# A decoder trunk on one core: the Strassen-like blocks of the down projection asked for earlier, spaced five groups apart, with VectorE's work cut smaller and the sums of h on GpSimd

## The reference

```python
g = x @ w_gate;  u = x @ w_up                    # 2048 -> 5632
gc = conv_b + sum(conv_w[j] * gp[:, j:j + S])    # three causal taps
y = (silu(gc) * u) @ w_down                      # h (256 x 5632) times w_down, 5632 -> 2048
x = layer_norm(ALPHA * x + y, ln2_g, ln2_b)
```

## Time and profile before

| | us |
|---|---|
| median of 3 runs | 2232.48 (2232.12 to 2232.66) |
| the profiled execution, its own time | 2233.07 |
| span of the profiled execution | 2231.0 |
| TensorE busy | 2204.4 |
| VectorE busy | 1531.2 |
| ScalarE busy | 1073.2 |
| GpSimd busy | 242.6 |

### The profile page before, as it was taken

How to read it: one execution, slowest core, us unless ns; L and a number is a source line. 1 busy time by engine, 2 the same in 40 slices (tenths; PEclk the granted TensorE clock), 3 DMA queues, 4 the chain that set the end, 5 groups by cost and what they waited for, 6 DMA issues and landing times.

```text
span 2231.0 us, 28589 instructions
## 1 busy us (share of the span) xinstructions
PE 2204.4 (99%) x11370; PEld 1882.7 (84%) x11370; DVE 1531.2 (69%) x2034; ACT 1073.2 (48%) x1405; POOL 242.6 (11%) x250
## 2 busy tenths in 40 slices
PE   9999999999999999999999999999999999999998
PEld 7888888888888888778888888888888888887787
DVE  6655676786667666787685566767866666677876
ACT  5444555444444445444354445554444444455443
POOL 1751000220000000000008410002200000000000
PEclk9999999999999999999999999999999999999999
DMA  8655565666666666656665554755666666666565
GB/s 276 194 169 161 152 217 176 184 190 191 189 191 190 191 189 210 195 170 198 209 193 169 162 165 146 226 177 182 189 189 189 190 190 190 191 216 194 162 199 186
DMA packets 210213, 420.94 MB, mean 189 GB/s; under 512 B 13056, under 2 KB 15136, under 8 KB 209056
## 3 DMA queue, kind: packets, MB, share of 16 engines
q1 hardware_dynamic: 207216, 406.37, 58.8%
q0 software_dynamic: 2432, 12.22, 1.6%
q10 hardware_dynamic: 432, 0.52, 0.1%
HBM read 416.97 MB, written 2.10 MB: 188 GB/s over the span
## 4 chain that ended last, share of the span: by engine, by line
PE 92%; DVE 5%; DMA 2%; issue 0%; SPq 0%; ACT 0%; POOLq 0%; POOL 0%; DVEq 0%
PE ps L1489 29%; PE ps L1493 15%; PE ps L1375 13%; PE ps L1377 13%; PE ps L1376 13%; DMA sraw<-in_w_down_dram 2%; DVE slo L1054 1%; DVE wlo L914 1%; PE ps L1539 1%; PE ps L1541 1%; PE ps L1540 1%; PE ps L1420 1%; PE ps L1638 1%; PE ps L1612 1%; DVE xres L1000 1%; PE ps L1589 1%
## 5 line engine op out<-in xcount | busy, mean ns | idle before, releaser
L914 DVE TENSOR_TENSOR wlo<-raw,whi 128x1024 fp32r<-128x1024 f32 x731 | 927.0, 1276 | 521.7 <-ACT whi L647 516.0
L647 ACT ACTIVATE whi<-raw 128x1024 fp32r<-128x1024 f32 x731 | 769.4, 1059 | 738.8 <-DMA raw<-in_w_up_dram 216.9
L1489 PE MATMUL ps<-xT,whi 128*128 128x512 f32 x2816 | 657.3, 390 | 0.0
L1489 PEld LDWEIGHTS ps<-xT,whi 128*128 128x128 f32 x2816 | 522.4, 188 | 104.5 <-ACT qkT L668 0.4
L1375 PE MATMUL ps<-whi,xT 128*128 128x512 f32 x920 | 369.0, 401 | 0.0
L1377 PE MATMUL ps<-whi,xT 128*128 128x512 f32 x920 | 359.1, 390 | 0.0
L1376 PE MATMUL ps<-wlo,xT 128*128 128x512 f32 x920 | 358.2, 389 | 0.0
L1493 PEld LDWEIGHTS ps<-xT,wlo 128*128 128x128 f32 x2816 | 350.5, 192 | 7.5
L1493 PE MATMUL ps<-xT,wlo 128*128 128x256 f32 x2816 | 352.8, 283 | 0.0
L1375 PE MATMUL ps<-whi,hT 128*128 128x512 f32 x552 | 216.3, 392 | 4.7 <-DVE wlo L914 4.7
L1376 PE MATMUL ps<-wlo,hT 128*128 128x512 f32 x552 | 216.1, 391 | 0.0
(11 more groups left out here) (237 smaller groups left out, 1587.3 us busy)
## 6 DMA issues: line engine op xcount, KB each, us to landing
raw<-in_w_gate_dram SPq DMA_DIRECT2D x176, 512.0 KB, 4.0
raw<-in_w_up_dram SPq DMA_DIRECT2D x176, 512.0 KB, 4.0
raw<-in_w_in_dram SPq DMA_DIRECT2D x175, 512.0 KB, 3.7
raw<-in_w_down_dram SPq DMA_DIRECT2D x140, 512.0 KB, 4.2
raw<-in_w_out_dram SPq DMA_DIRECT2D x64, 512.0 KB, 4.2
sraw<-in_w_down_dram SPq DMA_DIRECT2D x36, 512.0 KB, 4.8
xres<-in_x_dram POOLq DMA_DIRECT2D x4, 512.0 KB, 5.9
lnb<-in_ln_g_dram POOLq DMA_DIRECT2D x2, 1024.0 KB, 8.1
```

The costliest lines, as they stand in the source:

```text
L647: act.activation(whi[:, s, :, :], raw[:, s, :, :], ACT.Copy).then_inc(hi_done, 1)
L914: dve.tensor_tensor(wlo[:, s, :, :], raw[:, s, :, :], whi[:, s, :, :].bitcast(F32), ALU.subtract)\
L1489: return pe.matmul(ps[:, bank, :], whi[:, s, kk, m * P:(m + 1) * P], xT[:, kt, :, :].rearrange("p a s -> p (a s)"), start=kt == 0, stop=kt ...
```

## The change

- `SETS_AT`: blocks 0 to 4 behind groups 9, 14, 19, 24, 29; blocks 5 to 8 behind 38, 43, 48, 53.
- The two loads of `sraw` for a block no longer wait for all seven products of the block in front: kk=1 waits for two of them, kk=0 for four. For this `set_used` counts products, S3 comes before S1, and each load has a semaphore.
- VectorE: `set_sum` is two parts, at `at+1` and `at+2`; `set_low` is two parts, of 2 at `at+2` and of 5 at `at+3`. ScalarE: `form_high` and the first of set_high's parts go from `at` to `at+1`, the rest to `at+2` and `at+3`. T1, T3 wait until the block in front is done.
- The additions of the blocks' products come in three steps (4 additions; 2 statistics and 3 additions; 4 additions).
- `form_sums` goes from VectorE to GpSimd (its lines are the same; the diff below shows them only where they are added), where the five pairs' sums follow one another, each after `form_low` of the pair in front (`hform_lo`); the first after the last low half of h (`h_done`).

```diff
--- before.py
+++ after.py
@@ -40,7 +40,7 @@
 BASE_OUT = NC_IN * GC
 BASE_FFN = BASE_OUT + NC_OUT * GC
 BASE_DOWN = BASE_FFN + 2 * NC_FF * GC
-SETS_AT = ((11, 16, 20, 24, 28), (36, 41, 46, 51))
+SETS_AT = ((9, 14, 19, 24, 29), (38, 43, 48, 53))
 SETS = [(half, i) for half in range(2) for i in range(len(SETS_AT[half]))]
 SET_AFTER = [SETS_AT[half][i] for half, i in SETS]
 SET_LOAD = [-1] + SET_AFTER[:-1]
@@ -48,10 +48,14 @@
 DOWN = sum(HALF_GROUPS)
 DOWN_ENDS = [HALF_GROUPS[0] // 2, HALF_GROUPS[0], HALF_GROUPS[0] + HALF_GROUPS[1] // 2, DOWN]
 PREPARED = len(SETS_AT[0])
-PRODUCTS = ("A12", "S4", "A11", "S1", "S3", "S2", "A22")
-FACTORS = ("B21", "B22", "B11", "T1", "T3", "T2", "T4")
+SET_STEP = [max(a + 6, 8) for a in SET_LOAD]
+PRODUCTS = ("A12", "S4", "A11", "S3", "S1", "S2", "A22")
+FACTORS = ("B21", "B22", "B11", "T3", "T1", "T2", "T4")
+PER_SET = len(FACTORS)
+SUM_ORDER = ("T1", "T3", "T2", "T4")
+LAST_READ = (4, 2)
 SLOT = {"B11": 0, "B12": 1, "T3": 1, "B21": 2, "B22": 3, "T1": 4, "T2": 5, "T4": 6}
-TARGET = (0, 2, 4, 5, 7, 6, 1)
+TARGET = (0, 2, 4, 7, 5, 6, 1)
 SUMS = (((4,), (4, 6, 5)), ((4, 6, 7), (4, 6, 7, 5)))
 GROUPS = BASE_DOWN + DOWN
 
...
@@ -469,13 +473,13 @@
                         half, pair = SETS[k]
                         if k == 0:
                             wait_groups(sp, layer, BASE_DOWN)
-                        if layer + k > 0:
-                            sp.wait_ge(set_used, set_count(layer, k - 1))
                         for kk in (1, 0):
+                            if layer + k > 0:
+                                sp.wait_ge(set_used, PER_SET * (set_count(layer, k) - 2) + LAST_READ[kk])
                             row = (GK * pair + kk) * P
                             sp.dma_start(sraw[:, 2 * kk:2 * kk + 2, :].rearrange("p s n -> p (s n)"),
                                          w_down[layer, row:row + P, half * 2 * CW:(half + 1) * 2 * CW])\
-                                .then_inc(set_in, 16)
+                                .then_inc(set_in[kk], 16)
             rows = out.rearrange("b (t p) d -> (b t) p d", p=P)
             for t in range(TT):
 
@@ -518,6 +522,26 @@
                     link(ins)
                 else:
                     ins.then_inc(natural, 1)
+
+            def form_sums(layer, pair):
+
+                count = pair_count(layer, pair)
+                k0 = GK * pair
+                if pair == 0:
+                    wait_groups(pool, layer, BASE_DOWN)
+                    pool.wait_ge(h_done, layer * PAIRS + PAIRS)
+                if count > 1:
+                    pool.wait_ge(hform_lo, count - 1)
+                pool.tensor_tensor(hsum[:, :, :], hT[:, k0:k0 + GK, 0, :].bitcast(F32),
+                                  hT[:, k0:k0 + GK, 1, :].bitcast(F32), ALU.add).then_inc(hsum_done, 1)
+                pool.wait_ge(hsum_done, count)
+                a11, a21, a12, a22 = hsum[:, 0, 0:P], hsum[:, 0, P:SEQ], hsum[:, 1, 0:P], hsum[:, 1, P:SEQ]
+                pool.tensor_tensor(hform[:, 0, :], a21, a22, ALU.add).then_inc(hform_done, 1)
+                pool.tensor_tensor(hform[:, 3, :], a11, a21, ALU.subtract)
+                pool.wait_ge(hform_done, 3 * count - 2)
+                pool.tensor_tensor(hform[:, 1, :], hform[:, 0, :], a11, ALU.subtract).then_inc(hform_done, 1)
+                pool.wait_ge(hform_done, 3 * count - 1)
+                pool.tensor_tensor(hform[:, 2, :], a12, hform[:, 1, :], ALU.subtract).then_inc(hform_done, 1)
 
             def constants(layer):
 
@@ -616,8 +640,9 @@
                 for n in range(2 * PIECES):
                     affine_op(layer, n)
 
-                pool.wait_ge(h_done, layer * PAIRS + PAIRS)
-                pool.wait_ge(set_used, set_count(layer, len(SETS) - 1))
+                for pair in range(PREPARED):
+                    form_sums(layer, pair)
+                pool.wait_ge(set_used, PER_SET * set_count(layer, len(SETS) - 1))
                 carry_wait(pool, 3)
                 pool.dma_start(lnb2[:, 0, :], row(ln2_g, layer).broadcast_to([P, D_MODEL])).then_inc(ln2_in, 16)
                 pool.dma_start(lnb2[:, 1, :], row(ln2_b, layer).broadcast_to([P, D_MODEL])).then_inc(ln2_in, 16)
@@ -720,12 +745,14 @@
 
             def set_high(layer, k, part):
 
-                names = (FACTORS[0:2], FACTORS[2:5], FACTORS[5:7])[part]
-                for name in names:
-                    if name[0] == "T":
-                        act.wait_ge(set_sums, 4 * (set_count(layer, k) - 1) + ("T1", "T3", "T2", "T4").index(name) + 1)
-                    elif name == "B21":
-                        act.wait_ge(set_in, 32 * set_count(layer, k))
+                for i in ((0, 1), (2, 3, 4), (5, 6))[part]:
+                    name = FACTORS[i]
+                    if i == 0:
+                        act.wait_ge(set_in[1], 16 * set_count(layer, k))
+                    if i == 2:
+                        act.wait_ge(set_in[0], 16 * set_count(layer, k))
+                    if name in SUM_ORDER:
+                        act.wait_ge(set_sums, 4 * (set_count(layer, k) - 1) + SUM_ORDER.index(name) + 1)
                     act.activation(shi[:, SLOT[name], :], sraw[:, SLOT[name], :], ACT.Copy).then_inc(set_hi, 1)
 
             def form_high(layer, pair):
@@ -736,12 +763,11 @@
 
             def set_steps(layer, n):
 
-                for k, a in enumerate(SET_LOAD):
-                    if k < PREPARED and n == max(a + 6, 8):
+                for k, at in enumerate(SET_STEP):
+                    if k < PREPARED and n == at + 1:
                         form_high(layer, k)
-                    part = n - max(a + 6, 8)
-                    if 0 <= part < 3:
-                        set_high(layer, k, part)
+                    if 0 < n - at < 4:
+                        set_high(layer, k, n - at - 1)
 
             def ffn_chunk(layer, c, first):
                 for j in range(GC):
...
@@ -982,47 +1008,29 @@
                     last = dve.bn_stats(stats[:, t, c, :], xres[:, t, cols])
                 link(last)
 
-            def products(layer, c):
+            def add_products(layer, c, t):
 
                 cols = slice(c * CW, (c + 1) * CW)
                 if c % 2 == 0:
-                    for t in range(TT):
-                        wait_read(dve, layer, in_banks(c)[t], ("down", c))
-                for i in range(4):
-                    for t in range(TT):
-                        banks = SUMS[t][c % 2]
-                        if i >= len(banks):
-                            continue
-                        if i == 0 and c % 2 == 1:
-                            ins = dve.scalar_tensor_tensor(xres[:, t, cols], xres[:, t, cols], ALPHA,
-                                                           ps[:, banks[i], :], ALU.mult, ALU.add)
-                        else:
-                            ins = dve.tensor_tensor(xres[:, t, cols], xres[:, t, cols], ps[:, banks[i], :], ALU.add)
-                        link(ins)
-                if c % 2 == 1:
-                    for b in (4, 5, 6, 7):
-                        dve.nop().then_inc(psum_free[b], 1)
-                else:
-                    for t in range(TT):
-                        last = dve.bn_stats(stats[:, t, c, :], xres[:, t, cols])
-                    link(last)
-
...
             def form_low(layer, pair):
 
@@ -1032,50 +1040,61 @@
                 dve.tensor_tensor(third_form(pair)[:, 1, :], hform[:, 3, :], third_form(pair)[:, 0, :].bitcast(F32),
                                   ALU.subtract).then_inc(hform_lo, 1)
 
-            def set_sum(layer, k):
+            def set_sum(layer, k, part):
 
                 done = 4 * (set_count(layer, k) - 1)
-                dve.wait_ge(set_in, 32 * set_count(layer, k))
                 slot = lambda name: sraw[:, SLOT[name], :]
-                dve.tensor_tensor(slot("T1"), slot("B12"), slot("B11"), ALU.subtract).then_inc(set_sums, 1)
-                dve.wait_ge(set_sums, done + 1)
-                dve.tensor_tensor(slot("T3"), slot("B22"), slot("B12"), ALU.subtract).then_inc(set_sums, 1)
-                dve.tensor_tensor(slot("T2"), slot("B22"), slot("T1"), ALU.subtract).then_inc(set_sums, 1)
-                dve.wait_ge(set_sums, done + 3)
-                dve.tensor_tensor(slot("T4"), slot("B21"), slot("T2"), ALU.subtract).then_inc(set_sums, 1)
+                if part == 0:
+                    for kk in range(GK):
+                        dve.wait_ge(set_in[kk], 16 * set_count(layer, k))
+                    if layer + k > 0:
+                        dve.wait_ge(set_used, PER_SET * (set_count(layer, k) - 1))
+                    dve.tensor_tensor(slot("T1"), slot("B12"), slot("B11"), ALU.subtract).then_inc(set_sums, 1)
+                    dve.wait_ge(set_sums, done + 1)
+                    dve.tensor_tensor(slot("T3"), slot("B22"), slot("B12"), ALU.subtract).then_inc(set_sums, 1)
+                else:
```

(87 more changed lines are left out.)

1 line of the change is left out of this document (added).

## The result

The changed kernel takes 2260.03 us (median of 4 runs, 2257.28 to 2263.36) against 2232.57: 1.0123 times as long, 95% interval 1.0109 to 1.0137. It is slower, by 27.5 us; 2267 were predicted, in a range of 2233 to 2283. The profiled execution took 2263.36 with a span of 2261.5, 30.5 more than before.

The account below looks back on a forecast made before the run. TensorE was taken to bound the kernel, so only its stops count. Losses of 25.9 us a layer, 51.8 in two, less 20.6, plus 3.5 for the clock gave +34.7 on 2232.48: 2267 us, range 2233 to 2283.

Parts of the forecast that it names:

- block 0: First block of a layer: GpSimd's first sums of h make the forms and slo late, 4.1 us lost.
- blocks 1, 2, 3: Blocks beside GpSimd's sums: 2.0 us from VectorE's late chain plus 2.7 from GpSimd, 4.7 lost each.
- block 4: Late slo for products 0 and 2 and restarts, with no GpSimd sums beside it: 2.0 us lost.
- in front of block 5: Group 38's wlo stands behind y_chunk 1 on VectorE: 1.1 us late, in place of 4.3 lost before group 36.
- blocks 6 to 8: Second-half blocks: the second wlo waits for its own whi, 1.5 us lost each, 4.6 a layer.
- clock: TensorE falls to 1.2 GHz after long waits before blocks 0 to 3; mostly hidden, 0.4 for eight, +3.5 us in all.
- 20.6 us to win back: TensorE's loss from block 1's end to block 5's start, 10.4 + 10.2 us over two layers: all the change can win.
- The early loads earn nothing, since the sums stand behind a later wlo: Sraw loads arrive 2.4 to 3.4 us earlier, but sums move behind the wlo of at+1; nothing credited.
- X: Earliest start of the wlo of at+1 on VectorE, put at T+12.9; T is when TensorE ends the group before a block.
- GpSimd's sums run in that chain and take turns with VectorE's: From X on, GpSimd's additions delay VectorE by 1.9 us before slo 0 and 0.74 more before slo 2.
- Only the late chain: Rival, chance 0.20: GpSimd's sums fit VectorE's idle time or cost little; 2240 us, 2234 to 2252.
- Faster: Rival, chance 0.10: the long wait goes and blocks five apart suffice; loss 0 to 2 us, 2212 to 2215 us.

Follow-up runs that it names:

- e6: e5 with VectorE's and ScalarE's steps for block 5 moved behind the additions (steps 38 and 39, ScalarE from 37): 2212.56 us.
- e7: e5 with both loads of a block held until all seven products of the block in front are done: 2222.18 us.
- e1: The changed kernel with the sums of h back on VectorE at step at-1, the rest as changed: 2240.04 us.
- e5: e1 with the steps of VectorE and ScalarE at the places of the kernel before; spacing, early loads and additions in portions stay: 2220.81 us.
- e2: The changed kernel with GpSimd's sums of pair k held back until TensorE has done block k-1: 2242.82 us.
- e9: e1 with idle additions on GpSimd behind each form_low, one 128x512 and four 128x128, on a tile nobody else touches: 2254.86 us.
- e10: e1 with seven idle memsets of 128x512 on GpSimd behind each form_low, on a tile nobody else touches: 2239.52 us.
- e3: The kernel before with only the sums of h moved to GpSimd, started by form_low: 2253.82 us.
- e4: e2 with the steps of VectorE and ScalarE at the places of the kernel before: 2229.57 us.
- e8: The kernel before with the new SETS_AT list alone: 2222.56 us.

## Why the prediction was right

| term, us | predicted, a layer | layer 0 | layer 1 |
|---|---|---|---|
| block 0 | 4.1 | 2.2 | 2.7 |
| blocks 1, 2, 3 | 4.7 each | 6.3, 6.7, 3.6 | 6.0, 4.2, 3.6 |
| block 4 | 2.0 | 1.6 | 1.6 |
| in front of block 5 | 1.1 | 1.95 | 1.95 |
| blocks 6 to 8 | 4.6 | 4.8 | 3.7 |
| sum | 25.9 (and 1.8 clock) | 27.1 | 23.8 |

- *20.6 us to win back*: shown by e6, which loses none of it.
- *The early loads earn nothing, since the sums stand behind a later wlo*: right for the changed kernel, where in block 1 the weights landed at 905.64 and T1 started at 911.79. But e7 shows that with the steps at their old places the head start would have earned at most 1.4 us too: five groups are room enough without it. e1 against e5 (2240.0 and 2220.8) prices the places of the steps at 19 us. A raw load landed in 3.7 us, not the 4.1 that I took, so the chain began earlier: X was 14.8 us behind the end of group 9, and without block 0's lateness of 2.2 that is T+12.6 instead of T+12.9. Block 4 and the blocks of half 1 come out a little cheaper for it.
- *GpSimd's sums run in that chain and take turns with VectorE*: right in mechanism, shown by e2, e9 and e10. In block 1 TensorE started product 0 at X+7.9 and product 2 at X+10.7; the prediction had 8.25 and 11.33. The delay was 1.6 and 2.0 us, not 1.9 and 2.6. The big addition cost what was predicted (T2 takes 1.79 instead of 0.69: 1.1 against 1.18), the small ones less (0.13 to 0.26 longer for each T4, slo and wlo beside them, not 0.37). That is why block 3, which had neither a fall of the clock nor a late load, lost 3.6 instead of 4.7.
- *Block 0, 4.1 us*: too much. The forms were finished at 889.96 instead of 891.0; VectorE's sums ended at 889.10, and GpSimd's last addition took 0.46 with nothing beside it. The step itself was right: ScalarE waited 4.86 us for the forms. e2, which has the same first sums but nothing beside the later chain, loses 2.1 and 1.9 there.
- *The clock, 3.5 us in all*: too little. Blocks 1 and 2 of both layers, where it fell, cost 2.7, 3.1, 2.4 and 0.6 more than the 3.6 of block 3, where it stayed at 2.4 GHz. Of these 8.8 us 1.6 are not the clock's: the raw load in front of block 2 of layer 0 took 5.3 us instead of 3.7, and its first wait was that much longer. That leaves about 7.2. The slow matmuls outlasted the wait before product 2 that was to hide them: in block 1 of layer 0 they began only with product 2.
- *Group 38, 1.1*: measured 1.95. The step was right, VectorE's queue in front of it 0.85 us longer than added up.
- *The total is closer than its terms.* Blocks 0 and 1 to 3, without clock and late load, came out 9.9 us below what was added up, block 4 and blocks 6 to 8 another 1.5; the clock (by 3.7), group 38 (by 1.7) and the late load (1.6) came out above. So 51.0 stands against 55.3, and that the miss is no larger is partly luck. The median lies 3.3 below the profiled execution, which is the slowest of the four (mean granted clock 0.993 to 0.997). Of the likeliest case's span, the upper end follows from the bounds given for landings and clock; they add up to 2258 for the lower one, not 2253.
- *Rivals.* "Only the late chain" was put at 2240 us; e1, which is that case, took 2240.04. To the tenth that is luck: its blocks lost 1.6 to 1.8 instead of 2.0, and the group in front of block 5 1.95 instead of 1.1. "Faster" put 2212 to 2215 on all stalls gone, and said that VectorE would have to do its sums ahead of the wlo of `at+1`. e5 does that and takes 2220.81; the additions' stretch, which the rival took to be mended by the portions, still costs 3.6 us a layer and goes only in e6 (2212.56).

## What to carry to other kernels

An earlier load is worth nothing if its consumer also moves back in its engine's queue, or if the load was early enough already; look at where the first instruction that uses it stands, not at when it lands. An idle engine isn't free for work that reads SBUF beside VectorE: give it a start that falls into VectorE's idle time, and ask what event releases it, since here the release came from the very chain that had no slack. Ask too who waits for its result: in e3 and e4 it was ScalarE, with the next weight's high half behind it. When two queues of work (the additions of a half and the next block's preparation) fall on the same steps, portions didn't help here (3.6 us a layer in e5, with them; 3.6 and 4.7 in e8, without); moving one of them behind the other did.

## What the runs showed of the hardware

- VectorE and GpSimd did not always take turns, where both added from SBUF. In e4 GpSimd's 128x512 addition waited through VectorE's wlo one after another, 4.99 us in all; in e2 it did so for 4.15. At 118.67 us in the kernel before, and in the changed kernel, it got in behind the first. What decides it stays open.
- GpSimd's memset, which reads nothing, neither is held up nor disturbs VectorE (e10: 0.52 to 0.53 us each in all 70, and 2239.52 us against e1's 2240.04). The Trainium skill, SBUF — State Buffer, section Who interferes with whom, has both cases, additions that collide and writes that don't, and the traces agree.
- TensorE's clock followed waits of about 2 us in one place and not in another. In the changed kernel it was at 1.2 GHz 0.5 to 1.5 us after the end of waits of 1.98, 1.90 and 2.01 us and before the end of the one of 3.45, but it stayed at 2.4 after block 3's 1.88 and 1.03; in e1, with waits of at most 1.7, it stayed at 2.4 too, while in e3 it fell in blocks whose longest wait was 1.3. In front of block 5 e5 waited 2.45 and 2.44 us and kept 2.4 GHz both times (granted clock 1.00), e7 waited 2.45 twice and went to 1.2 both times (0.79 over the 8 us around), which is most of what e7 lost more there. The length of the wait alone doesn't decide it; what does stays open.
